# Second mixer of a two-block transformer kernel: softmax steps and weight splits in another order, activation tables loaded elsewhere

## The reference, cut to what matters

```python
def hybrid_layer(x, cos, sin, layer_idx, ...):          # second block, twice
    proj = rms_norm_2(x, attn_norm) @ w_in               # 1024 x 5444
    aq, ak, av, iq, ik, iw, bq, bk, bv, gates = split_cols(proj)
    # aq, ak, ik, bq, bk: rms norm a head, then rotary; iq: rotary
    ya = sparse_attention(aq, ak, av, iq, ik, iw, k_sel=64)   # 8 heads; keys chosen by an index score
    lam = exp(sum(dl[0] * dl[1])) - exp(sum(dl[2] * dl[3])) + lam_init
    yb = diff_attention(bq, bk, bv, lam)                 # 4 heads: softmax - lam * softmax
    yb = rms_norm_2(yb, b_subln) * (1 - lam_init)
    g_a, g_b = split(sigmoid(gates + gate_bias))
    x = x + (g_a * (ya @ w_up_a) + g_b * (yb @ w_up_b)) @ w_out
    gate, up = split(rms_norm_2(x, ffn_norm) @ w_ffn_in)
    return x + (silu(gate) * up) @ w_ffn_out
```

## Time and profile before

| | |
|---|---|
| median of 3 runs | 1848.74 us |
| the profiled execution's own time | 1847.19 us |
| its span, first to last instruction | 1845.5 us |
| mean granted TensorE clock | 0.999 of full |
| PE busy | 1792.5 us, 97% |
| DVE busy (VectorE) | 1123.2 us, 61% |
| ACT busy (ScalarE) | 936.9 us, 51% |
| POOL busy (GpSimd) | 195.0 us, 11% |
| DMA | 315 MB, 52.3% of 16 engines' span |

### The profile page before, as it was taken

How to read it: one execution, slowest core, us unless ns; L and a number is a source line. 1 busy time by engine, 2 the same in 40 slices (tenths; PEclk the granted TensorE clock), 3 DMA queues, 4 the chain that set the end, 5 groups by cost and what they waited for, 6 DMA issues and landing times.

```text
span 1845.5 us, 23629 instructions
## 1 busy us (share of the span) xinstructions
PE 1792.5 (97%) x8739; PEld 1458.1 (79%) x8739; DVE 1123.2 (61%) x1647; ACT 936.9 (51%) x1265; POOL 195.0 (11%) x226
## 2 busy tenths in 40 slices
PE   6999999999999999999999999999999999999999
PEld 4888887788888888877888877778888777788887
DVE  5555577655545555777555489766554688665553
ACT  5444475644444444665544376655444656745441
POOL 0000020000000000300000096100001382000000
PEclk9999999999999999999999999999999999999999
DMA  7656454455556554553555564445556544345551
GB/s 232 197 187 208 141 178 120 137 182 182 208 170 192 182 210 140 182 138 115 182 186 213 173 205 137 141 157 160 183 187 212 184 159 156 128 150 182 184 206 65
DMA packets 221017, 316.21 MB, mean 171 GB/s; under 512 B 14056, under 2 KB 162176, under 8 KB 220672
## 3 DMA queue, kind: packets, MB, share of 16 engines
q1 hardware_dynamic: 220928, 315.03, 52.3%
HBM read 313.94 MB, written 1.05 MB: 171 GB/s over the span
## 4 chain that ended last, share of the span: by engine, by line
PE 82%; DVE 7%; issue 3%; ACT 2%; DVEq 2%; POOL 1%; DMA 1%; SPq 1%; POOLq 0%; ACTq 0%
PE ps L1767 25%; PE ps L1769 24%; PE ps L1768 24%; DVE w_lo L1102 2%; PE ps L1872 2%; ACT w_hi L656 1%; PE ps L1777 1%; PE ps L1960 1%; PE ps L1948 1%; PE ps L1936 1%; PE ps L1905 1%; DVE score L1542 1%; DVEq L1545 1%; DVEq L1553 1%; PE ps L2240 1%
## 5 line engine op out<-in xcount | busy, mean ns | idle before, releaser
L1102 DVE TENSOR_TENSOR w_lo<-raw,w_hi 128x2048 fp32r<-128x2048 f32 (+1 forms) x298 | 674.1, 2284 | 250.0 <-ACT w_hi L656 248.7
L1767 PE MATMUL ps<-w_hi,aT_hi 128*128 128x512 f32 (+2 forms) x1728 | 689.2, 399 | 15.1 <-DVE aT_lo L1135 8.7
L1769 PE MATMUL ps<-w_hi,aT_lo 128*128 128x512 f32 (+2 forms) x1728 | 670.9, 388 | 0.0
L1768 PE MATMUL ps<-w_lo,aT_hi 128*128 128x512 f32 (+2 forms) x1728 | 668.9, 387 | 0.0
L656 ACT ACTIVATE w_hi<-raw 128x2048 fp32r<-128x2048 f32 (+1 forms) x298 | 556.8, 1900 | 184.8 <-PE ps L1769 178.8
L1767 PEld LDWEIGHTS ps<-w_hi,aT_hi 128*128 128x128 f32 x1728 | 325.4, 188 | 91.9 <-issue 23.7
L1769 PEld LDWEIGHTS ps<-w_hi,aT_lo 128*128 128x128 f32 x1728 | 325.1, 188 | 68.2
L1768 PEld LDWEIGHTS ps<-w_lo,aT_hi 128*128 128x128 f32 x1728 | 325.9, 189 | 59.6
L706 ACT ACTIVATE att<-ps,rstd 128x256 f32<-128x256 f32 x132 | 55.5, 472 | 377.8 <-PE ps L1769 377.7
L1176 DVE SCALAR_TENSOR_TENSOR att<-ps,rstd,att 128x256 f32<-128x256 f32 x132 | 57.8, 479 | 287.4 <-ACT att L706 287.4
L1767 PE MATMUL ps<-w_hi,gT_hi 128*128 128x512 f32 x528 | 207.1, 392 | 0.0
(11 more groups left out here) (260 smaller groups left out, 1393.3 us busy)
## 6 DMA issues: line engine op xcount, KB each, us to landing
raw<-in_w_in SPq DMA_DIRECT2D x120, 512.0 KB, 4.5
raw<-in_w_ffn_gate SPq DMA_DIRECT2D x88, 512.0 KB, 4.1
raw<-in_w_ffn_up SPq DMA_DIRECT2D x88, 512.0 KB, 5.1
raw<-in_w_ffn_down SPq DMA_DIRECT2D x88, 512.0 KB, 4.4
raw<-in_w_ffn_in SPq DMA_DIRECT2D x88, 512.0 KB, 4.9
raw<-in_w_ffn_out SPq DMA_DIRECT2D x44, 512.0 KB, 4.7
raw<-in_w_out SPq DMA_DIRECT2D x32, 512.0 KB, 4.7
raw<-in_w_ck SPq DMA_DIRECT2D x8, 512.0 KB, 3.9
```

What stands on the lines that cost most here:

```text
L1102: V.tensor_tensor(o, a, h, ALU.subtract).then_inc(units_split, 1)
L1767: M(o, ah, wh, start=start, stop=False)
L1768: M(o, ah, wl, start=False, stop=False)
L1769: return M(o, al, wh, start=False, stop=stop)
```

## The change

In the feed-forward, behind the last `keep`, ScalarE gets one square root of a constant into a scratch tile of its own. In the second mixer the lists of ScalarE and VectorE are put in another order: masks, exponentials and P stand in front of weight splits, item(0) and item(1) stand further forward, lambda's exponential and its two subtractions stand just ahead of the first softmax, the first sigmoid stands behind the last pair's exponentials and turned P, and one split of the output product behind `up_a`. In layer 1, unit 3 is split behind the root and the first evacuation on ScalarE, and behind `norm` on VectorE. TensorE's, GpSimd's and SyncE's lists stay as they are, and so does the arithmetic.

```diff
+        root_probe = sb("root_probe", [P, 1])
...
                 keep(FT - 1, FT - 1)
+                act.wait_ge(consts_ready, 1)
+                nc.scalar.drain()
+                nc.scalar.activation(root_probe[:, :], ident[:, 0:1], ACT.Sqrt)
                 for u in range(U_DOWN - 2):
                     split(st, p0 + U_UP + 2 + u)
...
                 else:
-                    turned_in(st, B, GAIN_ATTN + l * KC, l * 2 + 7, P2_WIN)
+                    stage(B, GAIN_ATTN + l * KC, PARTS[:2])
+                    square(l * 2 + 7, 0)
+                    split(st, 2)
+                    stage(B, GAIN_ATTN + l * KC, PARTS[2:], first=2)
+                    square(l * 2 + 7, 1)
+                    squared()
                     root(N)
...
                 evac(0)
-                if l == 0:
-                    split(st, 3)
+                split(st, 3)
                 head_squares(0)
                 win_split(2, 0)
                 head_roots(0)
-                act.wait_ge(lam_sums, l + 1)
-                nc.scalar.activation(lam[:, 0:2], lam[:, 0:2], ACT.Exp).then_inc(lam_exp, 1)
                 win_split(2, 1)
...
                 win_split(3, 0)
                 evac(1)
+                item(0)
                 head_squares(1)
                 win_split(3, 1)
                 head_roots(1)
-                item(0)
...
                 item(4)
                 win_split(6, 0)
+                act.wait_ge(lam_sums, l + 1)
+                nc.scalar.activation(lam[:, 0:2], lam[:, 0:2], ACT.Exp).then_inc(lam_exp, 1)
                 exps(0)
                 evac(4)
                 win_split(6, 1)
                 probs_turned(0)
+                exps(1)
                 split(st, P2_WIN + 14)
-                exps(1)
                 diff_out(0)
                 evac(5)
                 head_squares(4)
-                split(st, P2_WIN + 15)
                 item(6)
                 probs_turned(1)
                 head_roots(4)
                 exps(2)
+                split(st, P2_WIN + 15)
                 diff_out(1)
                 split(st, P2_WIN + 16)
                 evac(6)
                 probs_turned(2)
+                exps(3)
                 split(st, P2_WIN + 17)
-                exps(3)
                 diff_out(2)
                 item(8)
                 split(st, P2_WIN + 18)
                 probs_turned(3)
+                exps(4)
                 split(st, P2_WIN + 19)
-                exps(4)
...
                 split(st, P2_UP)
-                act.wait_ge(tile_done, W + 9)
-                gate(GATES2 + DM)
                 probs_turned(6)
+                exps(7)
                 split(st, P2_UP + 1)
-                exps(7)
                 diff_hi()
                 split(st, P2_UP + 2)
                 probs_turned(7)
+                act.wait_ge(tile_done, W + 9)
+                gate(GATES2 + DM)
                 split(st, P2_UP + 3)
```

In VectorE's list:

```diff
                 else:
-                    turned_in(st, B, GAIN_ATTN + l * KC, P2_WIN)
+                    split(st, 2)
+                    stage(B, GAIN_ATTN + l * KC, PARTS[2:], first=2)
                     norm(N)
+                    split(st, 3)
...
                 head_scales(0)
-                dve.wait_ge(lam_exp, l + 1)
-                V.tensor_tensor(lam[:, 2:3], lam[:, 1:2], lam[:, 0:1], ALU.subtract)
-                V.drain()
-                V.tensor_tensor(lam[:, 2:3], lam[:, 2:3], par2[:, 704:705], ALU.subtract)
                 win_split(2, 1)
                 win_split(3, 0)
+                item(1)
                 head_sums(1)
                 win_split(3, 1)
                 head_scales(1)
-                item(1)
...
                 head_scales(3)
-                best(1)
                 item(5)
                 best(1)
-                win_split(6, 0)
+                dve.wait_ge(lam_exp, l + 1)
+                V.tensor_tensor(lam[:, 2:3], lam[:, 1:2], lam[:, 0:1], ALU.subtract)
+                V.drain()
+                V.tensor_tensor(lam[:, 2:3], lam[:, 2:3], par2[:, 704:705], ALU.subtract)
                 masked(0)
                 best(1)
                 probs(0)
+                win_split(6, 0)
                 win_split(6, 1)
                 masked(1)
                 best(1)
-                split(st, P2_WIN + 14)
                 probs(1)
                 head_sums(4)
+                masked(2)
+                head_scales(4)
+                split(st, P2_WIN + 14)
+                probs(2)
+                item(7)
                 best(1)
                 split(st, P2_WIN + 15)
-                masked(2)
-                item(7)
-                head_scales(4)
                 best(1)
-                probs(2)
+                masked(3)
+                best(1)
+                probs(3)
                 split(st, P2_WIN + 16)
                 best(1)
...
-                masked(3)
+                item(9)
                 split(st, P2_WIN + 17)
-                item(9)
-                probs(3)
-                split(st, P2_WIN + 18)
...
+                masked(4)
                 gate(7, 0)
-                masked(4)
+                probs(4)
                 dve.wait_ge(tile_done, W + 7)
                 gate(7, 1)
+                split(st, P2_WIN + 18)
+                probs_turned(4)
                 split(st, P2_WIN + 19)
-                probs(4)
-                probs_turned(4)
                 masked(5)
                 gate(8, 0)
+                probs(5)
                 split(st, P2_WIN + 20)
                 gate(8, 1)
-                probs(5)
...
-                split(st, P2_WIN + 21)
                 probs_turned(5)
                 masked(6)
+                split(st, P2_WIN + 21)
                 dve.wait_ge(yb_root, l + 1)
                 V.reciprocal(ms[:, 0:8], ms[:, 0:8]).then_inc(yb_scale, 1)
+                probs(6)
                 gate(9, 0)
                 split(st, P2_UP)
-                probs(6)
...
                 up_b(1)
-                split(st, P2_OUT + 2)
                 up_a(1, 0)
                 up_a(1, 1)
                 stage(B + 6, parts=((0, 1), (1, 1)), first=2, banks=STAGE_BANKS_UP)
+                split(st, P2_OUT + 2)
                 split(st, P2_OUT + 3)
```

## The result

The changed kernel took 1851.84 us in the median of 20 runs (1850.43 to 1853.05), the kernel before 1848.77 (20 runs, 1846.62 to 1851.58). The ratio is 1.0018, with a 95% interval of 1.0012 to 1.0025: slower by 3.1 us, just inside the 0.2% that the prediction called no change. Forecast were 1832.4 us and a range from 1827.5 to 1841.5. The sign was wrong, and the time lies 10 us outside the range.

The account below looks back on a forecast made before the run. TensorE was busy 97% of the span, so time could come only from its stops or slow stretches. Gains of 6.85 us (layer 0) and 9.4 (layer 1), together 16.3 off the 1848.74 median, gave 1832.4 us, range 1827.5 to 1841.5.

Parts of the forecast that it names:

- slower: Rival, second mixers: pieces 12 to 14 wait behind masks and P, tile 6 waits; at 10 us a layer, 1852.5 us; chance 0.04.
- P ahead of the splits, pairs 4 to 7, and the output product: Second mixers' late part: waits at L1583 (2.4 us) and L1631 (0.6) go, pair 7 loses 0.35, each layer.
- The probe in the feed-forward: End of the gate/up loop: the probe's 1.5 us on ScalarE fit into 3.1 us of slack, cost 0.
- Root's load ahead of the mixer: Front of layer 0's second mixer: the root starts 0.5 us earlier, so the awaited weight subtraction is 0.5 earlier.
- The rotations: Stops at the transposes end with GpSimd's rotations, which start earlier: gain 1.1 us in layer 0, 2.2 of 2.4 in layer 1.
- a rival of its own, with 0.12: Rotations do not get earlier: GpSimd's start moves but meets more subtractions; 12.5 us off in all, 1836; chance 0.12.
- Exponentials against evac(4): TensorE's stop at tile 5 (L912) nearly goes: gain 1.55 us in layer 0, 2.4 plus 1.6 of low clock in layer 1.
- the prediction's own sign of being right: Sign for tile 5 of the second mixers: no wait for L912 over 0.6 us.
- Pairs 2 and 3: L1588's waits (1.8 and 2.2 us) come back as waits for item(8) and item(9); taken as 0.
- 22.7 - 1.2 + 1.75 + 1.45 = 24.7 us: VectorE's work from head_sums(4) to item(9) in the new order, 24.7 us; over 27 us was a sign of being wrong.
- The first rival: VectorE and GpSimd block each other: item(9) 2 to 4 us later a layer, 8 us off, 1840.5; chance 0.16.
- the early part: Everything in the second mixers ahead of pair 4, for which 10.1 us stood in the sum.

Follow-up runs that it names:

- the run with the tile at the end: Changed kernel with its scratch tile root_probe allocated behind all other tiles, nothing else different: 1841.27 us, ratio 0.9964 to the kernel before.
- the late part: Kernel before with only the change's reordering from masked(4) on, including the first sigmoid and the output product's split: 1843.57 us, ratio 0.9975.
- the last two: On the combined reorderings with up products' operands placed (1839.4 us): probs(0), probs(1) and diff_lo forward, 1830.58 us; then probs_turned(7) ahead of split(P2_UP + 2), 1828.74 us.
- items 8 and 9 forward: Changed kernel with root_probe allocated last, item(8) straight behind exps(3) on ScalarE and item(9) behind probs(3) on VectorE: 1837.99 us, ratio 0.9946.

## Why the prediction was wrong

**The missing term.** The change was costed instruction by instruction, and the probe by its 1.5 us of ScalarE. The tile it writes has a line of its own in the diff and had none in the sum. This is the step of the prediction that failed first: a term put at nothing without a reason. It measures +10.6 us (tile moved in the changed kernel) or +12.3 us (tile added to the kernel before). With it, even the forecast's 16.3 would have left 6; with the 6.6 us that the mixers gave, it turned the sign. No rival held it, "slower" least of all, whose 0.04 rested on another mechanism that did not occur: there is no wait for a low part of tile 6.

**Point by point, the mixers.**

- *P ahead of the splits, pairs 4 to 7, and the output product.* Right: 3.1 us a layer forecast, 2.95 measured. L1583's waits are gone, and pair 7 lost 0.4 at diff_lo where 0.35 stood.
- *The probe in the feed-forward.* Right: it is hidden, and its load is the 1.28 us of the earlier trace rows. The Trainium skill (ScalarE: Activation LUTs, What ACT_TABLE_LOAD costs) gives the load as much, and a drain of 1.38 us on top; that drain does not show here, the square root begins 0.02 us behind the load. ScalarE behind the last copy of a feed-forward:

```profile
152.73 1.28 ACT L727 ACT_TABLE_LOAD   x1
154.03 0.20 ACT L727 ACTIVATE root_probe<-ident 128x1 f32<-128x1 f32 x1
```

- *Root's load ahead of the mixer.* Right: 0.5 forecast, and L1110's wait fell from 1.6 to 1.1 us.
- *The rotations.* The failed step is "the rotation starts 1.1 to 1.9 us earlier". In layer 0 GpSimd came free later instead: its first rotation had met two weight subtractions before (2.40 and 2.38 us), and now met three, two of them back to back:

```profile
1082.02 2.40 POOL L589 TENSOR_TENSOR proj<-proj,rg 128x64 f32<-128x64 f32 x1
1084.39 2.37 POOL L590 TENSOR_TENSOR proj<-proj,rg 128x64 f32<-128x64 f32 x1
1086.90 0.32 POOL L595 TENSOR_TENSOR proj<-proj,rg 128x64 f32<-128x64 f32 x1
...
1091.52 1.27 POOL L589 TENSOR_TENSOR proj<-proj,rg 128x512 f32<-128x512 f32 x1 [0.18 <-issue]
```

  64 columns take 0.32 us alone and 2.4 beside a subtraction. The second rotation starts at 1091.52; less the 7.4 us by which this mixer begins later (the slower down products), that is 1084.1, where it was in the earlier trace rows. In layer 1, counted from the mixer's start in the run with the tile at the end, the first rotation did start 1.5 us earlier, but it ended only 1.2 us earlier in place of the 3 to 4 worked out, so 1.1 of the 2.4 us stayed, and two new stops of 0.5 and 0.3 us stand behind the rotations that follow. This was a rival of its own, with 0.12.
- *Exponentials against evac(4).* The step "item(5) is then done at 116.8 instead of 118.2" failed. It was done at 1126.13, or 1118.7 less the 7.4. The best that was taken out saved 1.5 us; but the last index score ended 1.7 us later (at 1116.25, or 1108.8 less the 7.4, against 1107.1), and the second step of head_sums(3) took 1.19 us instead of 0.65, both beside rotations, while TensorE came earlier. A wait of 0.6 us became one of 2.1, in layer 1 one of 0.3 became 1.8, and 1.2 us of the wait for evac(4) stayed there, where the prediction's own sign of being right was at most 0.6. I had priced the list with durations measured in other company.
- *Pairs 2 and 3.* Taken as zero, "1 us earlier to 2 us later"; measured 2.2 and 1.55 us later. The stop was foreseen ("1 to 3 us"), but its low clock was not in the term: I had one only from some 3 us up, and it came behind 2.55, 14 matmuls in 4 us at 0.57. The chain under it failed too: "22.7 - 1.2 + 1.75 + 1.45 = 24.7 us" from head_sums(4) to item(9) took 27.2 us in layer 0 (1145.37 to 1172.56), over the 27 that were named as the sign of being wrong. P of pair 2 now met the rotation of tile 5 and took 4.4 us, where it had taken 1.7; in layer 1 it took 3.6:

```profile
1152.24 2.08 DVE L1590 TENSOR_SCALAR att<-att,factor,lam 128x128 f32<-128x128 f32 x2
1154.40 2.29 DVE L1598 SCALAR_TENSOR_TENSOR att<-att,factor 128x128 f32<-128x128 f32 x2
```

  The mask of pair 3, for which the exponentials ahead of item(8) waited 5.5 us, stands behind it.

The first rival (VectorE and GpSimd block each other, 0.16) was, as far as the traces tell, the mechanism that ate most of the early part. Its price, 8 us, was near the 9.7 missing, and its rows were at hand; I gave it a sixth of the chance. The experiments show it directly only for P of pair 1 (4.9 us, then 1.5); for the rotations, item(5) and P of pair 2 of the changed kernel it is read from the trace.

What stays open: why a distance that is no multiple of 256 bytes costs these 6 ns, whether it is the distance to w_hi, to w_lo or to both, and how the little that the early part gave splits into its single moves, since only the late part was run alone.

## What to carry to other kernels

A diff's allocations are part of its cost: look up where every tile lies before and after, and where matmuls like these follow each other without a gap, keep their two operands a multiple of 256 bytes apart, or give a new scratch tile the last place. When an engine's list is reordered, write beside each call what the other engine of a sharing pair does at that moment; a P of 1.5 us beside a rotation took 4.9. And a wait that is removed is worth only the distance to the next late call: of the eight reorderings of the mixers tried on top of the change, four gave nothing over the fastest run that they were built from, and 10 of the 18 us came with the last two.

## What the runs showed of the hardware

- Matmuls of 128 x 512 in the fast 32-bit format follow each other at 227 ns or at 232 to 234 ns, at a granted clock of 1.00, according to the distance between the tiles they read: 227 at shifts of 0, 256 and 512 bytes, and where all tiles moved by 32 together; slow at 32, 64 and 128.
- The granted clock fell behind the stop of 2.55 us in layer 0, to 0.57 over 4 us. Behind a stop of 2.3 us at the same place of layer 1 it stayed at 1.00 in the changed kernel (1560 to 1564 us) and fell to 0.62 in the run with the tile at the end (1551 to 1555 us). It also fell behind shorter stops: to 0.57 over 4 us behind one of 1.8 us at pair_qk(0) of layer 1 (items 8 and 9 forward, 1507 to 1511 us), where the changed kernel had the same stop and kept 1.00. So the length of the stop alone does not decide.
- A one-column VectorE subtraction took 0.16 us where it began between two GpSimd operations and 1.17 beside one, a 64-column GpSimd product 0.32 alone and 2.4 beside a VectorE subtraction: the price of a meeting is the other's instruction, not one's own size. The Trainium skill (SBUF — State Buffer, SBUF: two separate sides) calls it a lock held for the whole instruction, and the trace agrees.
